# Latent columns projected features first, their norms by a product with ones, and the sample tokens of two heads side by side in both attentions

## The reference, cut to what matters

```python
h = rms_norm(x, p['norm_mix']); proj = h @ p['w_in']         # 1024 -> 2760 columns
u, z, a, b, cq, ckv, kpe = split(proj)                       # 1536, 512, 4, 4, 384, 256, 64
... causal_conv(u); gated delta rule in chunks of 64; o_gdn  # 4 heads of 128
c_q = rms_norm(cq, p['q_a_norm']); q = rms_norm(c_q @ p['w_qb'], p['q_norm']); rope on 64 of 192
lat_new = rms_norm(ckv, p['kv_a_norm'])                      # an output
kpe_new = rope(rms_norm(kpe, p['k_rope_norm']))              # an output
kv = concat(lat_past, lat_new) @ p['w_kvb']                  # keys and values of 4 heads
o_mla = block_causal_attention(q, k, v)                      # sample: 64 queries, 320 keys
x += concat(o_gdn, o_mla) @ p['w_out']
x += attention(rms_norm(h @ w_mq), mem_k, mem_v) @ p['w_mo'] # 4 heads, 256 memory tokens
x += moe(rms_norm(x))                                        # 32 experts of 1024, top 4
```

## Time and profile before

| what | value |
|---|---|
| median of 3 runs | 1306.26 us (1306.18 to 1307.25) |
| the profiled execution | 1307.44 us, span of its instructions 1305.5 us |
| TensorE busy | 1268.4 us, 97% of the span |
| VectorE, ScalarE, GpSimd busy | 466.9, 209.8, 21.7 us |
| mean granted TensorE clock | 0.997 |
| HBM traffic | 435.30 MB read, 3.33 MB written |

### The profile page before, as it was taken

How to read it: one execution, slowest core, us unless ns; L and a number is a source line. 1 busy time by engine, 2 the same in 40 slices (tenths; PEclk the granted TensorE clock), 3 DMA queues, 4 the chain that set the end, 5 groups by cost and what they waited for, 6 DMA issues and landing times.

```text
span 1305.5 us, 21010 instructions
## 1 busy us (share of the span) xinstructions
PE 1268.4 (97%) x8584; PEld 574.7 (44%) x8584; DVE 466.9 (36%) x988; ACT 209.8 (16%) x565; POOL 21.7 (2%) x35
## 2 busy tenths in 40 slices
PE   7999999999999999999999999999999999999997
PEld 5577655567553333333334333334333333333332
DVE  4455234533663333223333223333222233322233
ACT  2452233730430000000000000000000000000000
POOL 0000011100010000000000000000000000000000
PEclk9999999999989999999999999999999999999999
DMA  9611010771249999999999999999999999999996
GB/s 318 242 65 66 2 30 17 288 285 23 123 194 406 427 430 427 427 431 427 428 430 428 427 430 428 429 429 428 429 428 428 430 427 428 430 428 428 431 427 260
DMA packets 47869, 439.20 MB, mean 336 GB/s; under 512 B 7651, under 2 KB 10313, under 8 KB 23158
## 3 DMA queue, kind: packets, MB, share of 16 engines
q1 hardware_dynamic: 47596, 438.45, 80.6%
q10 hardware_dynamic: 234, 0.20, 0.1%
HBM read 435.30 MB, written 3.33 MB: 336 GB/s over the span
## 4 chain that ended last, share of the span: by engine, by line
PE 78%; DMA 16%; DVE 3%; ACT 1%; issue 1%; POOL 0%; SPq 0%; DVEq 0%; ACTq 0%; POOLq 0%
PE bank L1075 75%; DMA weights<-in_w_gu 15%; PE bank L1078 2%; ACT scaled L630 1%; DMA x<-in_x_sample 0%; POOL stats L591 0%; PE bank L1729 0%; DVE weights L1861 0%; DVE x L2441 0%; DVE x L2297 0%; ACT stream L630 0%; DVE stats L2218 0%; DVE scaled L1861 0%; DVE stream L2348 0%; DVE weights L1972 0%
## 5 line engine op out<-in xcount | busy, mean ns | idle before, releaser
L2441 DVE SCALAR_TENSOR_TENSOR x<-bank,small_weights,x 128x512 f32<-128x512 f32 (+1 forms) x192 | 134.8, 743 | 598.5 <-PE bank L1075 598.5
L1075 PE MATMUL bank<-weights,small_weights 128*64 128x512 f32 (+4 forms) x1456 | 336.1, 588 | 3.7 <-DMA weights<-in_w_gu 3.1
L1075 PEld LDWEIGHTS bank<-weights,small_weights 128*64 128x64 f32 (+1 forms) x1456 | 105.7, 139 | 196.1 <-issue 171.6
L1075 PE MATMUL bank<-weights,scaled 128*64 128x512 f32 x704 | 155.9, 595 | 5.1 <-ACT scaled L630 5.1
L1075 PE MATMUL bank<-scaled,small_weights 64*128 64x512 f32 x384 | 108.1, 640 | 1.4 <-DVE x L2441 0.7
L630 ACT ACTIVATE scaled<-scaled 128x512 f32<-128x512 f32 x32 | 20.1, 629 | 548.2 <-DVE scaled L1865 548.2
L630 ACT ACTIVATE scaled<-bank 128x512 f32<-128x512 f32 (+6 forms) x145 | 54.8, 406 | 323.0 <-PE bank L1075 241.8
L1075 PEld LDWEIGHTS bank<-weights,scaled 128*64 128x64 f32 x704 | 48.7, 137 | 97.1 <-issue 87.8
L1075 PE MATMUL bank<-stream,small_weights 128*64 128x512 f32 (+4 forms) x408 | 88.7, 544 | 1.5 <-DMA stream<-in_w_gu 1.1
L1075 PE MATMUL bank<-small_weights,weights 128*128 128x320 f32 (+3 forms) x320 | 87.6, 424 | 0.0
L1075 PE MATMUL bank<-small_weights 96*64 96x512 bf16 (+2 forms) x408 | 87.0, 499 | 0.0
(11 more groups left out here) (206 smaller groups left out, 899.1 us busy)
## 6 DMA issues: line engine op xcount, KB each, us to landing
weights<-in_w_gu SPq DMA_DIRECT2D x85, 2048.0 KB, 26.9
weights<-in_w_down SPq DMA_DIRECT2D x44, 2048.0 KB, 28.2
stream<-in_w_gu SPq DMA_DIRECT2D x21, 2048.0 KB, 28.0
more_weights<-in_w_gu SPq DMA_DIRECT2D x11, 2048.0 KB, 27.6
small_weights<-in_w_gu SPq DMA_DIRECT2D x11, 2048.0 KB, 26.1
small_weights<-in_w_down SPq DMA_DIRECT2D x10, 2048.0 KB, 28.1
more_weights<-in_w_down SPq DMA_DIRECT2D x10, 2048.0 KB, 28.3
weights<-in_w_in SPq DMA_DIRECT2D x3, 2048.0 KB, 16.3
```

Source lines behind the costliest of these rows:

```text
L1075: return pe.matmul(out, lhsT, rhs, start=start, stop=stop)
L2441: dve.scalar_tensor_tensor(xx, PS[bank][0:rows, :], gcur[0:rows, b:b + 1], xx, ALU.mult, ALU.add)\
```

## The change

Six edits, all in the dense part:

1. The latent columns cq and ckv (640) are projected features first: five ring products of 128 features by 320 tokens. The 64 kpe columns share one product with a and b (`ra` in the place of `ab`, 72 features), and are turned back to token rows by three transposes (`pe`).
2. ScalarE squares each latent product while it evacuates it; VectorE adds the squares over the feature blocks (`lq`), one product with a matrix of ones (`ls`) sums over the partitions and leaves the sum in all rows, ScalarE makes the reciprocal root of it by logarithm and exponential (a table set that must be loaded: `("tables", 2)` moves from before `k 0` to before `pj 19`), and VectorE scales five blocks in place.
3. `latents` has 15 transposes in place of 24: four and two for the cached latents and keys, three for kpe, six to turn the scaled latents for the output. They, and their waits, lie in another order.
4. The sample units of both attentions take two heads each: head h on partitions 0 to 63, h+1 on 64 to 127. Scores go to the two halves of the array; one maximum, exponential, normalisation and one set of transposes serve both; the value products stay one for each head. 12 units become 10.
5. The work between the steps moves to fit the shorter pipelines.
6. At the start VectorE squares block 0 and block 2, each in one instruction with a row sum; ScalarE squares block 1 only.

The loads change with it: w_in's kpe columns are a load of their own, earlier; one gain load on SyncE becomes one on ScalarE's queue; the w_out load also waits for the last q projection.

```diff
         RING = [("u", f) for f in (4, 5, 6, 7, 0, 1, 2, 3)] + [("ra", 0)] + [("u", f) for f in range(8, 12)] + \
             [("z", h) for h in range(NZ)] + [("cl", 0), ("cl", 1)] + [("vt", g) for g in range(3)] + \
-            [("cl", 2), ("cl", 3), ("clp", 0)]
+            [("pe", 0), ("cl", 2), ("cl", 3), ("ls", 0), ("cl", 4), ("ls", 1)]
...
-        for b in range(TB):
+        for b in range(2):
             for h in range(H):
...
+        for h in range(0, H, 2):
+            two = (h, h + 1)
+            mla_units.append(([[(qTn[:, j, qs], kT[:, j, ks]) for j in two], [(qTr[:, j, qs], kpeT[:, ks]) for j in two]],
...
-        CS_AT, WQ_AT, GO_AT = 2, 7, 8
+        CS_AT = 2
+        WQ_AT = {9: (0, 1), 10: (2, 3), 11: (4, 5), 12: (6, 7)}
+        GO_AT = {8: (0,), 9: (1,), 10: (2, 3), 11: (4, 5), 12: (6, 7)}
-        X2_AT, MO_AT, X3T_AT = 0, {8: (0, 0), 9: (0, 1), 12: (1, 0), 13: (1, 1)}, 11
+        X2_AT, MO_AT, X3T_AT = 0, {7: (0, 0), 8: (0, 1), 11: (1, 0), 12: (1, 1)}, 10
...
-                 ("q", 5, 0), ("q", 5, 1), ("q", 5, 2), ("pjb", 18), ("qg", 0), ("kd", 0),
-                 ("w", 0), ("w", 1), ("w", 2), ("pj", 19), ("pj", 20), ("pj", 21), ("a", 0), ("pj", 22), ("b", 0), ("pj", 23),
-                 ("out", 0), ("a", 1), ("pjm", 24), ("out_t", 0), ("b", 1), ("out", 1), ("kc", 0), ("a", 2), ("out_t", 1),
-                 ("norm", 1), ("b", 2), ("norm", 2), ("norm", 3), ("lat", 0), ("out", 2), ("a", 3), ("q", 0),
+                 ("q", 5, 0), ("q", 5, 1), ("q", 5, 2), ("pjb", 18), ("qg", 0), ("kd", 0), ("lq", 0),
+                 ("w", 0), ("w", 1), ("w", 2), ("tables", 2), ("pj", 19), ("pj", 20), ("pj", 21), ("a", 0), ("pj", 22), ("pj", 23),
+                 ("b", 0), ("lq", 1), ("pj", 24),
+                 ("out", 0), ("a", 1), ("pj", 25), ("pjm", 26), ("lq", 2), ("out_t", 0), ("b", 1), ("pj", 27), ("out", 1), ("kc", 0),
+                 ("a", 2), ("out_t", 1), ("norm", 1), ("norm", 2), ("b", 2), ("norm", 3), ("lat", 0), ("out", 2), ("a", 3), ("q", 0),
...
             def evacuate(pos):
+                elif kind == "ls":
+                    m = run(lat_rstd[i], src[:, 0:T], ACT.Ln, scale=1.0 / (Q_RANK, KV_RANK)[i], bias=eps_col)
...
+                    run(lat_sq[i % 2], src[:, 0:T], ACT.Square)
+                    m = run(lraw[:, i, :], src[:, 0:T])
                 m.then_inc(sem("pj_ev"), 1)
+                elif kind == "ls":
+                    act.wait_ge(sem("pj_ev"), pos + 1)
+                    run(lat_rstd[i], lat_rstd[i], ACT.Exp, scale=-0.5).then_inc(sem("ls_rstd"), 1)
...
             def latents():                                   # tensor
                 pe.wait_ge(sem("ld_wmk"), 16)
                 pe.wait_ge(sem("rows_ev"), NORM["mem"] + KD)
-                mem_project(wmk_sb, 0, 0, 2)
-                pe.wait_ge(*at("cq_ready"))
+                mem_project(wmk_sb, 0, 0, 1)
+                pe.wait_ge(sem("ld_state"), 64)
                 pe.wait_ge(sem("km_ev"), 2)
+                for k in range(2):
+                    for b in range(2):
+                        m = tr(PS[0][:, (2 * k + b) * P:(2 * k + b + 1) * P], lat_past[:, b, k * P:(k + 1) * P])
...
+                mem_project(wmk_sb, 0, 1, 3)
+                pe.wait_ge(*at("kpe_ready"))
...
+                pe.wait_ge(*at("lat_ready"))
+                for k in range(2):
+                    if k == 0:
+                        pe.wait_ge(sem("lat_ev"), 2)
+                    else:
+                        mem_project(wmk_sb, 0, 3, 5)
+                        pe.wait_ge(*at("kpe_ev"))
...
+                mem_project(wmk_sb, 0, 5, KD)
...
                 for n in range(len(units) + 3):              # tensor, attention
-                        for t, (q, k) in enumerate(terms):
-                            m = mm(PS[n % 2][0:rows, 0:nkeys], q, k, t == 0, t == len(terms) - 1)
+                        for t, sides in enumerate(terms):
+                            for side, (q, k) in enumerate(sides):
+                                m = mm(PS[n % 2][part(side, len(sides)), 0:nkeys], q, k, t == 0, t == len(terms) - 1)
...
+            def latent_sum(i):                               # vector
+                dve.wait_ge(sem("pj_ev"), ring_at("cl", (1, 2, 4)[i]) + 1)
+                if i == 1:
+                    dve.wait_ge(sem("lq_add"), 1)
+                tt(lat_rstd[i // 2], lat_rstd[0] if i == 1 else lat_sq[1], lat_sq[0], ALU.add).then_inc(sem("lq_add"), 1)
...
-            link(tt(x_junk[2][0:DEC, :], x3[0:DEC, 2, :], x3[0:DEC, 2, :], ALU.mult))
-            dve.tensor_reduce(ssq[0:DEC, 2:3], x_junk[2][0:DEC, :], AX, ALU.add).then_inc(mark("x2_sq"), 1)
+            for b in (0, 2):
+                rows = P if b < 2 else DEC
+                dve.wait_ge(sem(f"ld_x{b}"), 16)
+                dve.scalar_tensor_tensor(x_junk[b][0:rows, :], x3[0:rows, b, :], 1.0, x3[0:rows, b, :], ALU.mult, ALU.mult,
+                                         accum_out=ssq[0:rows, b:b + 1]).then_inc(mark(f"x{b}_sq"), 1)
```

More of the change, by code:

```diff
@@ L648, in feature_major @@
                     .then_inc(sem("rows_ev"), 1)
-            for b in range(2):
-                act.wait_ge(sem(f"ld_x{b}"), 16)
-                run(x_junk[b], x3[:, b, :], ACT.Square, accum_out=ssq[:, b:b + 1]).then_inc(mark(f"x{b}_sq"), 1)
+            act.wait_ge(sem("ld_x1"), 16)
+            run(x_junk[1], x3[:, 1, :], ACT.Square, accum_out=ssq[:, 1:2]).then_inc(mark("x1_sq"), 1)
             act.wait_ge(sem("ld_head"), 16)
@@ L952, in attention @@
                     if n < len(units):
-                        rows, terms, nkeys, masked, vs, out = units[n]
+                        terms, nkeys, masked, vs, out = units[n]
                         act.wait_ge(sem("att_mx"), ATT[tag] + n + 1)
@@ L956, in attention @@
                             act.wait_ge(sem("att_tr"), ATT[tag] + n - 1)
-                        run(prob[0:rows, n % 2, 0:nkeys], PS[n % 2][0:rows, 0:nkeys], ACT.Exp, scale=scale,
-                            bias=amx[0:rows, n % 2:n % 2 + 1], accum_out=asum[0:rows, n % 2:n % 2 + 1])\
+                        run(prob[:, n % 2, 0:nkeys], PS[n % 2][:, 0:nkeys], ACT.Exp, scale=scale,
+                            bias=amx[:, n % 2:n % 2 + 1], accum_out=asum[:, n % 2:n % 2 + 1])\
                             .then_inc(sem("att_ex"), 1)
                     if 2 <= n <= len(units) + 1:
-                        rows, terms, nkeys, masked, vs, out = units[n - 2]
+                        terms, nkeys, masked, vs, out = units[n - 2]
                         u = n % 2
@@ L1167, in project @@
                     return
+                if kind == "pe":
+                    for b in range(TB):
+                        rows = P if b < 2 else DEC
+                        m = tr(bank[0:rows, ROPE * b:ROPE * (b + 1)], raT[0:ROPE, b * P:b * P + rows])
+                    m.then_inc(sem("pj_mm"), 1)
+                    return
+                if kind == "ls":
+                    pe.wait_ge(sem("lq_add"), 2 + i)
+                    mm(bank[:, 0:T], ones, lat_rstd[i]).then_inc(sem("pj_mm"), 1)
+                    return
                 for k in range(k0, k1):
@@ L1503, in attention, with part @@
             def attention(tag, units, between, behind=None):
+                def part(side, sides):
+                    return slice(0, P) if sides == 1 else half(side)
                 for n in range(len(units) + 3):
@@ L1522, in attention @@
                             pe.wait_ge(sem("att_pt"), ATT[tag] + n - 3)
-                        for t, v in enumerate(vs):
+                        for t, v in enumerate(vs[0]):
                             kr = v.shape[0]
-                            m = tr(PS[2 + u][0:kr, t * P:t * P + rows], prob[0:rows, u, t * P:t * P + kr])
+                            m = tr(PS[2 + u][0:kr, t * P:(t + 1) * P], prob[:, u, t * P:t * P + kr])
                         m.then_inc(sem("att_tr"), 1)
                     if n >= 3:
-                        rows, terms, nkeys, masked, vs, out = units[n - 3]
+                        terms, nkeys, masked, vs, out = units[n - 3]
                         u = (n - 3) % 2
@@ L1532, in attention @@
                             pe.wait_ge(sem("att_o"), ATT[tag] + n - 4)
-                        for t, v in enumerate(vs):
-                            kr = v.shape[0]
-                            m = mm(PS[4 + u][:, 0:rows], v, probT[0:kr, u, t * P:t * P + rows], t == 0, t == len(vs) - 1)
+                        for side, values in enumerate(vs):
+                            cols = part(side, len(vs))
+                            for t, v in enumerate(values):
+                                m = mm(PS[4 + u][:, cols], v, probT[0:v.shape[0], u, t * P + cols.start:t * P + cols.stop],
+                                       t == 0, t == len(values) - 1)
                         m.then_inc(sem("att_pv"), 1)
```

299 lines of the change are left out of this document (137 added, 162 removed).

## The result

The changed kernel takes 1297.45 us (median of 4 executions, 1296.48 to 1298.88), the kernel before 1306.29 us (median of 4, 1306.18 to 1307.25). By the medians it is 8.8 us faster; the ratio is given as 0.9926 with a 95% interval of 0.9913 to 0.9939, which is 9.7 us (8.0 to 11.4). The direction was right and the size was not.

A forecast was written before the change was run, and what follows sets the result against it. TensorE's chain sets the first release of a tile buffer (391.65 us); a fixed DMA stream of 914 us follows. Terms sum to -4.85 us, taking the 1306.26 us median to 1301.4; range 1299.2 to 1303.5, for 8 in 10 1298.0 to 1304.3.

The forecast's parts named there:

- start: Sample rows' squares at the kernel's beginning: row sum in the same instruction starts the next stage 1.15 us earlier.
- `ra` in the place of `ab`: Product shared by kpe with a and b: streams the same 320 columns, so it gives nothing.
- latent products: Latent columns features first: 26.3 us before, 24.5 after; taken as -1.7 us, bounds -1.2 and -2.1.
- table load: ScalarE's load before the first value-token copy delays that copy, TensorE's third group and `a 0`: +0.7 us.
- wait at `kc`: TensorE's cached-key transposes must wait for ScalarE's logarithm behind `ls 1`: +0.85 us, bounds 0 and +1.2.
- `latents`: Nine transposes fewer give -1.25 us, but TensorE idles 1.5 us for rotated kpe: net +0.15 us.
- first attention: Paired sample units save scores, transposes, gaps and switches: -3.6 us, bounds -2.5 and -4.2.
- second attention, to the first refill: Removed work mostly becomes new idleness, router 0.4 us nearer, VectorE then sets the pace: -0.1 us.
- (a): Rival, chance 0.12: predicted waits are covered, or second attention gives its removed work in full, or both; called 1298.4 us.
- (b): Rival, chance 0.06: the array's halves do not run side by side for scores, as weight loads alternate; 1305.0 us.
- (c): Rival, chance 0.04: the end does not follow the first release, from a slower stream or unfinished preloads; 1306.3 us.
- (d): Rival, chance 0.04: new idleness around 343 and 356 us brings TensorE's clock down to 1.2 GHz; about 1309.5 us.

The follow-up runs named there:

- run 1: The kernel before with only the two-head sample units in both attentions and the moves between steps that go with them; 1302.22 us, ratio 0.9958.
- run 4: The kernel before with the memory rows' transposes issued behind the sample product, not between its steps; 1307.62 us, ratio 0.9988.
- run 5: The kernel before with the memory transposes between full-width latent product steps and the sample product alone; 1305.78 us, kernel before beside it 1308.28.
- run 6: The changed kernel with ScalarE's table load behind the kpe squares, not ahead of the first value-token copy; 1297.90 us.
- run 7: The changed kernel with the cached keys' transposes behind scan step a 2, not in front of it; 1296.92 us.
- run 8: The changed kernel with VectorE's norm and rotation of kpe behind a 1, not at the end of its queue before the new latents; 1295.06 us.
- run 3: The kernel before with the latent columns features first, without the start edit or the paired units; 1305.43 us, ratio 0.9980.
- run 2: The kernel before with only the start edit: VectorE squares blocks 0 and 2 with a row sum in the same instruction; 1305.50 us, ratio 0.9987.

## Why the prediction was right and wrong

What bounds the kernel was right: the end followed the first release to 0.2 us, and TensorE's own chain set that release. The waits that it named are there too. What failed are the sizes of terms, two above all. Each term against what the traces and runs give for it:

| term | forecast | measured |
|---|---|---|
| start | -1.15 | -1.24 |
| `ra` in the place of `ab` | 0 | -0.30 |
| latent products | -1.7 | -3.16 |
| table load | +0.7 | +0.84 |
| wait at `kc` | +0.85 | +0.73 |
| `latents` | +0.15 | -0.11 |
| first attention | -3.6 | -4.04 |
| second attention, to the first refill | -0.1 | -1.47 |
| sum | -4.85 | -8.75 |

The measured sum stands beside 8.8 us by the medians, within the interval of 8.0 to 11.4. The start is taken from the pair 2.59 and 1.35 us. The latent products are -0.85, +0.01 and -2.87 of the table of offsets with 0.55 for `ls 1`, and `kc` is 1.28 less this 0.55. The second attention is -1.52 with the +0.05 behind it; run 1 gives -1.23 for the same.

**The largest miss is the latent products: 1.5 of the 3.9 us.** The step that failed is the count of 26.3 us before against 24.5 after: the sample product's "eight steps of 0.79 us" were set against a full-width product at 4.58, and the sixteen memory transposes between the steps were left at their price. The trace before held both numbers: 0.79 us for the product's share of a step, 0.37 for the pair of transposes behind it. The pair costs 0.22 between full-width steps, a price that the trace before held too (180.82 to 181.04 us, among the turns of the latents); 8 times 0.15 is 1.2 us of the miss, and the full-width step beside them, 0.54 and not 4.58 / 8 = 0.57, is 0.24. Runs 4 and 5 show that the alternation makes both dear. Why the array wants this time is not shown; only that it is spent when instructions on column halves and full-width ones follow each other.

**The second attention: 1.4 us.** The step that failed is the sum "-0.76 + 1.3 - 1.75 + 0.8 = -0.4" and the one behind it, "the last output product ends where it did". Windows of the same stretch, from the surroundings of the first output product to the router, kernel before and changed kernel:

```profile
342.90:367.51 24.61, 24.12 (x97) 12.72 (x96) 10.36 (x39) 8.28 (x25) 0.89 (x2) 1.00 0.00 1
```

```profile
336.14:359.23 23.09, 21.87 (x94) 12.42 (x93) 8.42 (x29) 6.97 (x19) 1.94 (x9) 1.00 0.01 1
```

TensorE's busy time falls from 24.12 to 21.87, 2.25 us and not 1.75; of the 0.50 between them 0.33 is in the sample units' value products, which the sum left out (2.11 us for four, 1.78 for two pairs, in TensorE's timelines). Its idleness rises from 0.49 to 1.22, 0.73 us, where the sum had 0.54 (-0.76 + 1.3) and 0.8, so 1.34. The first output product came where it was forecast (336.98 is 343.74 with the offset of 6.76, forecast 343.75), with 0.84 us of idleness in front of it for the 1.0 forecast. The second idle place, behind ScalarE's square, was put at 1.1 us and is 0.38. So the router came 1.53 us nearer and not 0.4. Then 0.3 of the forecast 0.4 was struck out because VectorE "sets the pace" behind the last output product. In the changed kernel 0.05 of 1.52 us was lost there. That VectorE absorbs nothing there is shown only to within the scatter of that stretch (24.06 to 25.01 us).

**The first attention** was 0.44 us short. TensorE's two timelines can be added up from the filler in front of the first pair to the one behind the last value product (261.40 to 279.49 us before, 258.68 to 272.73 after; a filler is a piece of the output product). The scores gave 2.71 us and the transposes 0.60, as forecast. The eight fillers gave 0.59: alone one takes 0.63 to 0.74 us, and two in a row, as six of them now stand, 1.08 or 1.18. The value products gave 0.20 and the idleness took 0.06. Against these 0.73 us the forecast allowed 0.2 for "gaps and switches".

**The waits** were right to 0.3 us, each in its place, and runs 6 to 8 removed each by removing the named cause. The table load starts as the copy before it ends (138.38), and the copy behind it starts 1.30 us later, so the load's own 1.28 us is all that it took on ScalarE. The Trainium skill (ScalarE: Activation LUTs, What ACT_TABLE_LOAD costs) puts about 1.38 us of drain on top of a load; by an estimate from it this term would be +2.1. The trace shows +0.84, and run 6 takes back 0.84.

**`ra`** was set at nothing since it streams the same 320 columns. The pair of products around it took 8.78 us in each trace with the edit and 8.98 in each without; 72 features cost 0.2 us less than 8, and the step in front of the pair another 0.10 (1.08 us, not 1.18). No run tells why.

**The rivals.** (a) gave 1298.4, nearest to the measured time, but by the wrong way: none of its waits was covered. It was half right in that the second attention gives more of its removed work. Its nearness to 1297.45 is luck. (b) is refuted by eight score instructions in 1.37 us, (c) by 913.7 against 913.9 us. (d) did not come where it was placed. The granted clock did fall in single executions, at 273 us in run 3 and near 250 us in runs 2, 4 and 6, in kernels with and without the edits. The range was too narrow on this side for two reasons. The latent products came out beyond their own bound (-3.16, bound -2.1), and `ra` had none. Both attentions stayed within theirs, but missed on the same side, where the range took the bounds as not all at one end.

## What to carry to other kernels

When a product that alternates with other instructions is replaced, price the whole step from one start to the next on both sides. The instructions in between change their cost with their neighbour. When two steps of a software pipeline go, write down busy time and idle time as two separate sums; idleness is then checked place by place, since here one place was right and the other three times too large. Small pieces of work that are put between steps change their price too, when two of them come to stand together. Waits that a change creates are cheap to move once they are named: four reorderings of a hand-written chain, none of which touched the arithmetic, gave another 3.75 us by the offsets, 4.6 by the medians.

## What the runs showed of the hardware

- A step of four instructions on the two column halves costs 0.66 us alone and 0.79 when it alternates with full-width transposes; a pair of these costs 0.37 there and 0.22 between full-width steps.
- Between the same marks, up to the router, the dense part repeats to 0.01 us from execution to execution. The scatter of this kernel (1305.2 to 1317.3 us on one chip) has other places: the landing of the first rows (7.65 to 9.19 us), the moment from which TensorE runs at full pace (19.4 and 21.0 us in the first two traces, 16 to 19 in the five that record it as a step of the clock), stretches at 1.2 GHz in the middle, and the stretch from the router to the first refill (24.06 to 25.01 us). Windows of run 2 show one such stretch behind a loosely filled one:

```profile
248.00:250.00 2.00, 1.19 (x11) 0.96 (x11) 1.69 (x6) 1.07 (x6) 0.00 (x0) 1.00 0.94 332
250.00:252.00 2.00, 2.00 (x9) 1.45 (x10) 1.22 (x6) 1.39 (x6) 0.00 (x0) 0.51 0.90 300
```

  In run 3 it fell while TensorE was busy without a gap, and neither of the first two traces has such a stretch there. What decides it stays open.
- VectorE's row sum in the same instruction costs a read of 0.08 us (10.34 in the changed kernel's start); ScalarE's, behind its square of block 1 in the same trace, costs 0.19.
- Two fillers of the first attention in a row take 1.08 us, one alone 0.64.
